# Last three projections of a hybrid decoder layer: seven half-size block products in place of eight, token-major, with the merged rows kept on chip

## The reference, cut to what matters

```python
h = rms_norm(x, norm_w)
proj = h @ w_in                    # q|k|v, z, beta, alpha of branch A; q|k|v, z of branch B; gates
oa = gated delta rule(...) * silu(z_A)     # 8 heads x 128
ob = block attention(...)  * silu(z_B)     # 8 heads x 128
merged = sigmoid(g_A) * (oa @ w_out_gdn) + sigmoid(g_B) * (ob @ w_out_moba)
x = x + merged @ w_o
```

## Time and profile before

| | us |
|---|---|
| median of 3 runs (1697.09 to 1698.97) | 1698.05 |
| span of the profiled execution | 1695.3 |
| TensorE busy in that span | 1669.0 |
| VectorE, ScalarE, GpSimd busy | 777.0, 623.8, 109.3 |

### The profile page before, as it was taken

One profiled execution on the slowest core, in us unless ns is written; L12 is line 12 of the kernel. 1 busy time (PEld: TensorE's weight loads), 2 busy tenths in 40 slices (PEclk: granted clock), 3 DMA queues, 4 the chain that ended last, 5 costly groups with the idle time before them and its releaser, 6 DMA issues.

```text
span 1695.3 us, 21115 instructions
## 1 busy us (share of the span) xinstructions
PE 1669.0 (98%) x8233; PEld 1385.5 (82%) x8233; DVE 777.0 (46%) x1001; ACT 623.8 (37%) x825; POOL 109.3 (6%) x113
## 2 busy tenths in 40 slices
PE   6999999999999999999999999999999999999997
PEld 5888888888888888888888878888888888888886
DVE  5745646656456457455465453233322323352221
ACT  5434434435335345344343353223322222341110
POOL 4000001000001000000000100000000000000000
PEclk9999999999999999999999999999999999999999
DMA  8214223232143032232232353543443344452332
GB/s 252 75 37 119 58 74 87 74 80 80 49 105 80 25 105 80 57 97 73 59 100 59 82 179 81 131 110 82 108 116 97 80 130 108 139 182 82 130 135 100
DMA packets 251368, 165.31 MB, mean 98 GB/s; under 512 B 5731, under 2 KB 235334, under 8 KB 250694
## 3 DMA queue, kind: packets, MB, share of 16 engines
q1 hardware_dynamic: 245606, 144.90, 31.3%
q0 software_dynamic: 5728, 19.93, 3.2%
HBM read 152.76 MB, written 12.06 MB: 97 GB/s over the span
## 4 chain that ended last, share of the span: by engine, by line
PE 93%; DMA 2%; DVE 2%; ACT 1%; issue 1%; SPq 0%; POOL 0%; POOLq 0%; ACTq 0%
PE bank L437 21%; PE bank L441 20%; PE bank L439 20%; PE bank L466 6%; PE bank L848 4%; PE bank L849 4%; PE bank L847 4%; PE bank L877 2%; PE bank L880 2%; PE bank L879 2%; DMA w_raw<-in_w_o_dram 2%; PE bank L471 1%; PE bank L628 1%; PE bank L644 1%; ACT w_hi L915 1%
## 5 line engine op out<-in xcount | busy, mean ns | idle before, releaser
L437 PE MATMUL bank<-h_hi,w_hi 128*128 128x512 f32 x1520 | 620.8, 408 | 0.0
L441 PE MATMUL bank<-h_hi,w_raw_r 128*128 128x512 f32 x1520 | 595.5, 392 | 0.0
L439 PE MATMUL bank<-h_lo,w_hi 128*128 128x512 f32 x1520 | 593.5, 390 | 0.0
L1269 DVE TENSOR_TENSOR w_raw_r<-w_raw,w_hi 128x2048 fp32r<-128x2048 f32 x128 | 293.4, 2292 | 409.7 <-ACT w_hi L915 408.5
L915 ACT ACTIVATE w_hi<-w_raw 128x2048 fp32r<-128x2048 f32 x128 | 244.7, 1912 | 428.1 <-PE bank L441 188.5
L441 PEld LDWEIGHTS bank<-h_hi,w_raw_r 128*128 128x128 f32 x1520 | 285.3, 188 | 61.8
L437 PEld LDWEIGHTS bank<-h_hi,w_hi 128*128 128x128 f32 x1520 | 286.1, 188 | 56.2 <-issue 1.9
L439 PEld LDWEIGHTS bank<-h_lo,w_hi 128*128 128x128 f32 x1520 | 286.4, 188 | 55.1 <-issue 1.9
L877 PE MATMUL bank<-w_hi,h_hi 128*128 128x512 f32 x256 | 99.9, 390 | 1.6 <-DVE w_raw_r L1269 1.6
L847 PE MATMUL bank<-o_split,w_hi 128*128 128x512 f32 x256 | 100.9, 394 | 0.0
L848 PE MATMUL bank<-o_split,w_hi 128*128 128x512 f32 x256 | 100.9, 394 | 0.0
(11 more groups left out here) (270 smaller groups left out, 1597.4 us busy)
## 6 DMA issues: line engine op xcount, KB each, us to landing
w_raw<-in_w_in_dram SPq DMA_DIRECT2D x96, 1024.0 KB, 6.0
w_raw<-in_w_o_dram SPq DMA_DIRECT2D x16, 1024.0 KB, 10.4
w_raw<-in_w_out_gdn_dram SPq DMA_DIRECT2D x16, 512.0 KB, 7.3
w_raw<-in_w_out_moba_dram SPq DMA_DIRECT2D x16, 512.0 KB, 7.1
x_tiles<-in_x_dram SPq DMA_DIRECT2D x4, 1024.0 KB, 10.0
act_raw<-branch_outputs POOLq DMA_DIRECT2D x4, 1024.0 KB, 8.5
x_residual<-in_x_dram SPq DMA_DIRECT2D x4, 1024.0 KB, 7.1
out_dram<-out_tiles POOLq DMA_DIRECT2D x16, 256.0 KB, 4.5
```

The lines of the kernel that those rows point to most:

```text
L437: pe.matmul(PJ[slot % 2][:], w_hi[slot % 2][:, c], h_hi[:, k, :], start=(k == 0), stop=False, skip_group_check=True)
L439: pe.matmul(PJ[slot % 2][:], w_hi[slot % 2][:, c], h_lo[:, k, :], start=False, stop=False, skip_group_check=True)
L441: mm = pe.matmul(PJ[slot % 2][:], w_lo[slot][:, c], h_hi[:, k, :], start=False, stop=(k == KT - 1), skip_group_check=True)
L1269: dve.tensor_tensor(w_lo[slot][:], raw[slot][:], w_hi[slot % 2][:].bitcast(F32), ALU.subtract)\
```

## The change

Stages 2 and 3 are written anew, stage 1 keeps its work (some tiles move, some semaphores are shared; the last head is taken out of the loops).

A "quad" is a product of all 512 tokens by 1024 columns: 4 quads for the gates, 2 for each branch, 2 for `w_o`. Both operands are cut in 2x2 blocks (256 tokens, half the rows, 512 columns), and the quad is seven block products (`P11, P12, PS1, PS2, PS4, PS3, P22`) in Winograd's form instead of eight. Four of them need sums of activation blocks (S1, S2, S4, S3) and four need sums of weight blocks (T1 to T4). The activations are stationary, the weights move (token-major). A "unit" is 2 k-tiles x 512 columns of one product, 12 matmuls (2 token tiles x 2 k-tiles x 3); a quad has 7 x 4 units (7 x 2 for the branches, which have half the rows), 224 units in all. ScalarE makes the hi part (`op_hi`) and VectorE the lo part (`op_lo`) of each unit, 128x1024, into a ring of four; `op_hi(n)` waits until unit n - 4 has been multiplied.

- GpSimd forms T1 to T4 in place, 128x1024 per instruction: 16 per quad of four units, 8 per quad of two, 128 in all. Before this stage it also makes S3 of h in three steps of 128x2048 (`own_s3`), and later that of the merged rows in two (`merged_s3`).
- VectorE makes the other sums and the lo parts of all of them: of h 7 steps and 4 parts of 128x2048, of the two branches 8 steps and 14 parts of 128x1024, of the merged rows 2 steps of 128x1024, 4 of 128x2048 and 7 parts of 128x2048. ScalarE makes the hi parts.
- Out of PSUM: ScalarE copies 4 x 2 tiles of 128x512 per quad to a block in SBUF, VectorE adds another 4 x 2 from PSUM to them (`block_add`). Gates are clamped (128x1024), made sigmoids and stored to DRAM; the output of branch A is multiplied by its gate, read back, and stored; that of branch B is multiplied by its gate, and A's part, read back, is added.
- Each merged block is then turned by 8 transposes on TensorE (8 blocks, 64 transposes) and copied by ScalarE into the place of h. The merged rows no longer go through DRAM.
- Weight blocks are loaded 0.5 MB at a time; some blocks are loaded again, so a quad of four units takes 24 such loads.

```diff
+HALF = T // 2
+COLS = 512
+UK = 2
+UNIT = UK * COLS
+RINGS = 4
+P11, P12, PS1, PS2, PS4, PS3, P22 = range(NP)
+SOURCE = (SLOT_A, SLOT_C, SLOT_B, SLOT_B, SLOT_C, SLOT_A, SLOT_C)
+G_QUADS, Y_QUADS, W_QUADS = 4, 4, 2
+Y0, YB, W0 = G_QUADS, G_QUADS + 2, G_QUADS + Y_QUADS
+LEAD = RINGS
+
+def ku(q):
+    return 2 if Y0 <= q < W0 else 4
...
+            load_first(0)
+            load_third(0)
+            load_second(0)
+            for q in range(NQ):
+                quad_loads(q)
...
+            def form_t1(q):
+                for j in range(ku(q)):
+                    pool.wait_ge(op_loaded[SLOT_A][j], op_loads(q, j, SLOT_A, 0))
+                    pool.wait_ge(op_loaded[SLOT_B][j], op_loads(q, j, SLOT_B, 0))
+                    pool.tensor_tensor(ops[:, SLOT_B, j, :], ops[:, SLOT_B, j, :], ops[:, SLOT_A, j, :], ALU.subtract)\
+                        .then_inc(s["t_formed"], 1)
+            def form_t2(q):
+                for j in range(ku(q)):
+                    pool.wait_ge(op_loaded[SLOT_C][j], op_loads(q, j, SLOT_C, 1))
+                    pool.wait_ge(s["op_lo"], unit(q, PS1, j) + 1)
+                    pool.tensor_tensor(ops[:, SLOT_B, j, :], ops[:, SLOT_C, j, :], ops[:, SLOT_B, j, :], ALU.subtract)\
+                        .then_inc(s["t_formed"], 1)
...
+            def own_s3():
+                pool.wait_ge(s["win_done"], N1)
+                pool.wait_ge(s["a_step"], 2)
+                pool.tensor_tensor(a21, a21l, a11l, ALU.subtract).then_inc(s["a3_step"], 1)
+                pool.wait_ge(s["a3_step"], 1)
+                pool.tensor_tensor(a21, a21, a21h, ALU.add).then_inc(s["a3_step"], 1)
+                pool.wait_ge(s["a3_step"], 2)
+                pool.tensor_tensor(a21, a21, a11h, ALU.subtract).then_inc(s["a3_step"], 1)
...
+            form_t1(0)
+            own_s3()
+            for q in range(NQ):
+                if q > 0:
+                    store_block(q - 1, 3)
+                form_t2(q)
+                if q == W0:
+                    merged_s3()
+                form_t3(q)
+                store_block(q, 0)
+                form_t4(q)
+                if q + 1 < NQ and q + 1 != W0:
+                    form_t1(q + 1)
+                store_block(q, 1)
+                store_block(q, 2)
+                if q + 1 == W0:
+                    form_t1(q + 1)
...
+            def product_unit(q, p, j):
+                n = unit(q, p, j)
+                if j == 0:
+                    product_waits(q, p)
+                    left_waits(q, p)
+                pe.wait_ge(s["op_lo"], n + 1)
+                for t in range(2):
+                    ps = bank[2 * PAIR[p] + t]
+                    for kk in range(UK):
+                        k = UK * j + kk
+                        c = slice(kk * COLS, (kk + 1) * COLS)
+                        a_hi, a_lo = left(q, p, k, t)
+                        pe.matmul(ps[:], a_hi, ring_hi[:, n % RINGS, c], start=(FRESH[p] and k == 0), stop=False,
+                                  skip_group_check=True)
+                        pe.matmul(ps[:], a_hi, ring_lo[:, n % RINGS, c], start=False, stop=False,
+                                  skip_group_check=True)
+                        mm = pe.matmul(ps[:], a_lo, ring_hi[:, n % RINGS, c], start=False, stop=(k == kn - 1),
+                                       skip_group_check=True)
+                mm.then_inc(s["pe_unit"], 1)
...
+            def op_hi(n):
+                q, p, j = place(n)
+                if n < LEAD:
+                    act.wait_ge(s["ma_mm"], 3 * H)
+                else:
+                    act.wait_ge(s["pe_unit"], n - LEAD + 1)
+                if p in (P11, P12, PS4):
+                    act.wait_ge(op_loaded[SOURCE[p]][j], op_loads(q, j, SOURCE[p], (P11, P12, PS4).index(p) // 2))
+                else:
+                    act.wait_ge(s["t_formed"], formed(q, (PS1, PS2, PS3, P22).index(p), j))
+                act.activation(ring_hi[:, n % RINGS, :], ops[:, SOURCE[p], j, :], ACT.Copy).then_inc(s["op_hi"], 1)
...
+            def op_lo(n):
+                q, p, j = place(n)
+                dve.wait_ge(s["op_hi"], n + 1)
...
+                dve.tensor_tensor(ring_lo[:, n % RINGS, :], ops[:, SOURCE[p], j, :],
+                                  ring_hi[:, n % RINGS, :].bitcast(F32), ALU.subtract).then_inc(s["op_lo"], 1)
...
+            op_lo(1)
+            own_step(1)
+            own_step(2)
+            own_step(3)
+            zclamp(last, 1)
+            op_lo(2)
             softmax_max(last, 0)
+            zmul(last, 1)
+            op_lo(3)
+            softmax_norm(last, 0)
             softmax_max(last, 1)
+            op_lo(4)
...
+            for n in range(8, N_UNITS):
+                q, p, j = place(n)
+                op_lo(n)
+                for qb in range(NQ):
+                    for pb in range(NP):
+                        if n == ended(qb, pb) + LEAD - 1:
+                            if qb >= W0 and pb in (P11, PS1, PS2, PS3):
+                                residual(qb, pb)
+                            if pb in BLOCK_PRODUCT:
+                                block_add(qb, BLOCK_PRODUCT.index(pb))
+                if q == 0:
+                    if (p, j) == (PS1, 1):
+                        own_step(6)
...
+                elif n == unit(W0, PS1, 0):
+                    merged_step(18)
+                elif n == unit(W0, PS1, 1):
+                    merged_step(19)
+                elif n == unit(W0, PS1, 2):
+                    merged_step(20)
```

More of the change, by code:

```diff
@@ new lines, with unit, ended, formed @@
+NQ = W0 + W_QUADS
+BLOCK_E, BLOCK_ROW, BLOCK_COL = (0, 2, 1, 0), (0, 0, 1, 1), (0, 1, 1, 0)
+BLOCK_PRODUCT = (P12, PS4, PS3, P22)
+LEAD = RINGS
+def ku(q):
+    return 2 if Y0 <= q < W0 else 4
+def unit(q, p=0, j=0):
+    return sum(NP * ku(i) for i in range(q)) + p * ku(q) + j
+def ended(q, p):
+    return unit(q, p, ku(q) - 1) + 1
+def formed(q, i, j):
+    return sum(4 * ku(b) for b in range(q)) + i * ku(q) + j + 1
+def op_loads(q, j, slot, nth):
+    quads = sum(j < ku(b) for b in range(q))
+    before = (1, N1 // RING, 1)[slot]
+    return 16 * (before + (2, 1, 3)[slot] * quads + nth + 1)
@@ new lines, in load_third, with load_again_a @@
+            def load_third(q):
+                for j in range(ku(q)):
+                    if q == 0:
+                        sp.wait_ge(s["win_done"], N1 - 1 + j // 2)
+                    else:
+                        sp.wait_ge(s["op_lo"], unit(q - 1, P22, min(j, ku(q - 1) - 1)) + 1)
+                        if j >= ku(q - 1):
+                            sp.wait_ge(s["y_sum"], 2 * 4 - 1)
+                    load_op(q, SLOT_C, 0, 1, 0, j)
+            def load_again_a(q):
+                for j in range(ku(q)):
+                    sp.wait_ge(s["t_formed"], formed(q, 0, j))
+                    sp.wait_ge(s["op_lo"], unit(q, P11, j) + 1)
+                    load_op(q, SLOT_A, 1, 0, 1, j)
@@ L431, in _ @@
+            store_block(NQ - 1, 3)
+            for e in range(3):
+                pool.wait_ge(e_stored[e], stored(NQ - 3, (3, 2, 1)[e]))
         @block.tensor
@@ L900, in _ @@
+            for n in range(N_UNITS):
+                q, p, j = place(n)
+                product_unit(q, p, j)
+                attention_tail(n)
+                for i in range(4):
+                    for qb in (YB, YB + 1):
+                        if n == ended(qb, BLOCK_PRODUCT[i]) + 2:
+                            merged_turn(qb, i)
         @block.scalar
@@ new lines, in _, with copy_out @@
+            head(last, last - 1)
+            def copy_out(q, p):
+                e = {P11: 0, PS1: 1, PS2: 2, PS3: 0}[p]
+                act.wait_ge(s["pe_unit"], ended(q, p))
+                if p == PS3:
+                    if q < YB:
+                        act.wait_ge(e_stored[0], stored(q, 0))
+                    else:
+                        act.wait_ge(s["yT_mm"], 4 * (q - YB) + 1)
+                elif q > 0:
+                    i = (3, 2, 1)[e]
+                    if q - 1 < YB:
+                        act.wait_ge(e_stored[e], stored(q - 1, i))
+                    else:
+                        act.wait_ge(s["yT_mm"], 4 * (q - 1 - YB) + i + 1)
+                for t in range(2):
+                    act.activation(E[e][:, t, :], bank[2 * PAIR[p] + t][:], ACT.Copy).then_inc(s["e_copy"], 1)
@@ L1193, in _ @@
+            op_hi(0)
+            op_hi(1)
+            evac(last, 7)
+            op_hi(2)
+            zsig(last, 1)
+            op_hi(3)
             softmax(last, 0)
-            zsig(last, 1)
+            op_hi(4)
             softmax(last, 1)
+            sums_hi(OWN, PS1)
             pTc(last, 0)
+            op_hi(5)
             softmax(last, 2)
             pTc(last, 1)
+            op_hi(6)
             softmax(last, 3)
-            def gate_sigmoid(u, which, count):
-                act.wait_ge(s["g_evac"], count + 1)
-                sigmoid(sg[:, u, which, :], s["g_sig"], 3 * count)
```

965 lines of the change are left out of this document (600 added, 365 removed).

## The result

The changed kernel takes 1760.68 us (median of 4 runs, 1760.19 to 1762.38) against 1697.95 before (1697.09 to 1698.97): ratio 1.0374, 95% interval 1.0361 to 1.0386. The forecast was 1708 with a range to 1742; the direction was right, the size was not. The profiled run spans 1758.5 us.

What follows compares the result with a forecast made beforehand. TensorE, busy 1669.0 of 1695.3 us, was taken as the bound. 1695.3 - 92.1 + 8 - 2 + 1.5 = 1610.7 without stalls, plus 95 of stalls is 1705.7 of span, forecast as 1708 us; range 1662 to 1742.

Steps and rivals of the forecast that it cites:

- The pitch and the count of matmuls: New stage on TensorE: 2688 matmuls instead of 3072, 0.2268 us each, 609.6 us instead of 701.7, so -92.1.
- ScalarE at nothing: ScalarE's copies and sigmoids, 47 of 76.2 us in a gate quad, were forecast to cost no time.
- the port: SBUF port pair shared by VectorE and GpSimd: two-SBUF-input VectorE instructions and GpSimd instructions exclude each other, so their times add.
- the duration of the forms: GpSimd's 1024-column weight-block sums: costed at 2.25 us; expected in the profile at 2.35 alone, 3.4 or more behind VectorE.
- Rival 1: The port pair binds, but half as much: stalls of 30 to 70 us, 1645 to 1685 us, faster; 25%.
- rival 2: GpSimd works beside VectorE without exclusion, so nearly all of TensorE's saving is kept: 1615 to 1640 us, faster; 8%.
- Rival 3: GpSimd's queue, not the port: store, T2, op_hi and TensorE wait in turn: 1740 to 1790 us, slower; 12%.
- the stalls: TensorE's waits: 31 us in quad 0, 2 in quads 1, 2, 37 in quads 3 to 7, 27 in quad 8; 97, taken as 95.
- 1610.7: Whole kernel's span in us without stalls: 1695.3 - 92.1 + 8 - 2 + 1.5.
- 664: Forecast demand in us on the port pair over the whole stage, more than TensorE's 623.
- chains across engines: Bounds of the forecast: idle time from uncounted chains across four engines, 5 to 8% of some 300 us, +20.
- a low clock after the gaps: Sign that the forecast is wrong: a clock below full level after TensorE's gaps in quad 0.

Runs made afterwards that it cites:

- e1: The changed kernel with GpSimd's T1 to T4 forms cut to 8 of 1024 columns, the rest of the sums left out: 1659.5 us.
- e4: The changed kernel with all 128 forms and five long A-side steps moved from GpSimd to VectorE, order set anew: 1707.6 us.
- e3: The changed kernel with GpSimd's store of the last head's output moved from ahead of the first T1 forms to behind them: 1758.95 us.
- e9: The changed kernel with VectorE's block additions in quads 4 to 7 and ScalarE's sixth-product copy two units behind instead of three: 1754.0 us.
- e2: The changed kernel with 312 unread filler matmuls in TensorE's known idle places in quads 0, 3 to 5 and 8: 1766.2 us.
- e5: The changed kernel with the next quad's block loads put ahead of gate loads in SyncE's queue: 1760.9 us.
- e8: e4 with the queue order of e5, and T3, T4 forms and sixth-product A-side steps later on VectorE in quads 0 and 8: 1703.6 us.

## Why the prediction was right and wrong

**Right.** The pitch and the count of matmuls (quad 9 in 76.6 us); ScalarE at nothing, which ended none of TensorE's large waits; that the port is the main cost, and in which quads; the duration of the forms. The trace agrees with the rule of the page "SBUF — State Buffer" of the Trainium skill, section "SBUF: two separate sides", that the loser fully blocks: the median of the T2 forms is 3354 ns where alone they take 2374. The estimate of 2.35 for a form from the page "GPSIMD Engine Reference" of the Trainium skill, section 3.1, was the better one for a form alone: two in a row start 2.31 apart.

**Rival 1** was refuted in its size, **rival 2** in its mechanism (e1, e4). **Rival 3** has the measured time in its range, 1740 to 1790. Its mechanism isn't what made most of it: quads 1 to 3 lose some 19 us without it, and e1 and e4 give them back. But it isn't nothing either. A store that waits, a T2 behind it, a hi part behind T2 and TensorE behind that is the 15.90 us gap of e3, and in the changed kernel T1 of quad 0 starts 23 us late behind the same store. How much of the 52 us below is this no run shows, since e3 moved the store and left its wait in the queue.

**The step that failed** is the stalls: 149 for 97. All else was within a few us, so the sum 1610.7 + 95 = 1705.7 misses by these 52. What the runs put in its place:

- *The load.* An instruction that is followed by one of its own engine costs a little more than I took: starts are 1.14 apart for a 1024-column instruction of VectorE, not 1.09, and 2.31 on GpSimd, not 2.25; the clamps take 0.69, the 2048-column ones 2.2 and 4.49. With these 664 becomes 128 x 2.31 + 5 x 4.49 + 272 x 1.14 + 22 x 2.2 + 16 x 0.69 = 688. That is the upper end. Where a form and a lo part alternate, the forms start 3.35 apart, and my 2.25 + 1.09 = 3.34 was right:

```profile
1706.75 13.43 POOL L596 TENSOR_TENSOR operands<-operands 128x1024 f32<-128x1024 f32 x4
```

- *What was left out.* I summed the port, but it is VectorE's own queue that makes the lo parts, and its 96 additions from PSUM stand in it too. In the trace of after they are 51.1 + 10.2 = 61 us. In quads 5 to 7 I put 8 us each on and took up to 5.5 off again where GpSimd could work beside them; in quads 3, 4 and 8 I never put them on (5.1, 5.1 and 10.2 us).
- *The order.* The late additions cost 6.7 (e9). The store ahead of T1 in quad 0 stands outside the forecast too: I had the forms there at 981, and they start at 1004.

By quads the 52 are 27 in quads 3 to 7, 10 in quad 8, 9 in quad 0 and 7 in quads 1 and 2.

How much a us of load is worth can be estimated from two runs. e1 takes 128 x 2.31 = 296 us of port time away for 101 us of time; e4 takes 128 x 1.17 + 5 x 2.3 = 161 away for 53. That is a third in both, but only as an average over the stage: for the 30 forms of quads 4 to 7 e1 gives 34 us for 69, e4 3 us for 35. By this third, 0 to 24 us of price and 37 to 53 us of additions missing in my load are some 12 to 26 us, with the order 19 to 32 of the 52. The rest, 20 to 33, isn't pinned to a cause; the wait in GpSimd's queue is one that stays open, and I had allowed 20 for chains across engines in the bounds, and none in the sum.

I named a low clock after the gaps as a sign that I was wrong. It came, but as a consequence: e2 removed half of it and gained nothing. Of the waits, 22.5 us were ended by VectorE's additions and not by lo parts, which I hadn't named.

The forms on GpSimd are most of what turned the change into a loss. With the same arithmetic on VectorE, where a form takes half as long, and with the orders of e5, e8 and e9, of which only the last gave much (13.7 us), it is a small gain.

## What to carry to other kernels

Where a tuned kernel's bound engine gives up work, add up the queue that has to feed it per stage: every instruction of that engine, those from PSUM too, and on top every instruction of the engine that shares its port. Handing work to the other engine at a shared port is no relief when it is the slower of the two there (2.31 us against 1.14 for the same 1024 columns). Follow the other engine's queue as well: a store that waits there holds back all that stands behind it, and moving it a few places only moves the gap. And before chasing a low clock beside a full engine, ask whether the engine would be ready any sooner without it.

## What the runs showed of the hardware

- The two engines don't take turns strictly. GpSimd, with instructions that had nothing to wait for, kept VectorE's 1.2 us lo part out for 11.26 us (the rest of one form, two whole ones and a 2048-column step, back to back); with VectorE at work, GpSimd's 4.49 us step took 12.52 (e3). It ended 4.5 us after VectorE had turned from lo parts to additions from PSUM at 1018.45, so it was let in there, and the clamp that VectorE began at 1019.77 took 3.78 us.
- A one-input VectorE instruction between SBUF tensors (128x1024 clamp) is stretched by GpSimd as well: 694 to 1841 ns, against 693 to 698 without it. The page "SBUF — State Buffer" of the Trainium skill, section "Who interferes with whom", lists `tensor_scalar` among the instructions that can take the shared pair, and the runs agree; I had counted the clamps' time, but not that they are shut out.
- After a gap of 13.94 us TensorE's granted clock was at 1.2 GHz (matmuls 0.43 us apart) for a dozen matmuls, then back at 2.4 GHz; with fillers in such gaps the stage's mean rose from 0.93 to 0.98.
